# The norm ahead of a short convolution, with its root taken out of the matrix product: a two-block model on one Trainium2 core

## The reference, cut to what matters

```
def rmsnorm(x, w):
    y = x * rsqrt(mean(x * x, axis=-1) + 1e-6)
    return y * w

def shortconv_layer(h, w_in, conv_w, w_out):          # h is rmsnorm(x, norm_w[1])
    gate_b, gate_c, u, z = split(h @ w_in, 4, axis=-1)
    y = gate_b * causal_depthwise_conv(gate_c * u, conv_w)      # three taps
    return (y * silu(z)) @ w_out                                # added to x

x = x + hybrid_layer(rmsnorm(x, norm_w[0]), ...)
x = x + shortconv_layer(rmsnorm(x, norm_w[1]), ...)
return rmsnorm(x, final_norm_w)
```

## Time and profile before

| | |
|---|---|
| median of 3 runs | 3177.91 us (3171.27 to 3179.65) |
| the profiled execution: time, span | 3177.86 us, 3176.0 us |
| granted TensorE clock, mean | 0.982 |
| PE busy over the span | 2973.5 us (94%) |
| DVE, ACT, POOL busy | 2127.7 us (67%), 1550.3 us (49%), 87.7 us (3%) |
| HBM over the span | 171 GB/s |

### The profile page before, as it was taken

One profiled execution on the slowest core, in us unless ns is written; L12 is line 12 of the kernel. 1 busy time (PEld: TensorE's weight loads), 2 busy tenths in 40 slices (PEclk: granted clock), 3 DMA queues, 4 the chain that ended last, 5 costly groups with the idle time before them and its releaser, 6 DMA issues.

```text
span 3176.0 us, 53423 instructions
## 1 busy us (share of the span) xinstructions
PE 2973.5 (94%) x20420; PEld 2675.5 (84%) x20420; DVE 2127.7 (67%) x3042; ACT 1550.3 (49%) x2155; POOL 87.7 (3%) x113
## 2 busy tenths in 40 slices
PE   6989999987999998999799999999997899999998
PEld 6978888875988887777789999999997788888887
DVE  5766666665567778888666766776675665666655
ACT  4444444432455555777544544554453444444443
POOL 0000000000000000000000000000001000000000
PEclk9999999998999999999899999999998999999999
DMA  5423333320678887999434444444442455555554
GB/s 197 149 90 119 121 115 117 120 77 25 170 240 271 271 264 267 341 326 368 151 128 146 156 141 139 149 148 141 142 160 82 153 185 179 185 184 184 183 183 138
DMA packets 232514, 548.09 MB, mean 173 GB/s; under 512 B 17280, under 2 KB 99456, under 8 KB 232320
## 3 DMA queue, kind: packets, MB, share of 16 engines
q1 hardware_dynamic: 230240, 539.54, 51.4%
q0 software_dynamic: 1936, 5.64, 0.7%
q10 hardware_dynamic: 144, 0.19, 0.0%
HBM read 540.05 MB, written 2.10 MB: 171 GB/s over the span
## 4 chain that ended last, share of the span: by engine, by line
PE 63%; issue 26%; DVE 8%; ACT 3%; POOL 0%; DVEq 0%; ACTq 0%; POOLq 0%
PE gp L506 13%; PE gp L493 11%; PE gp L494 10%; PE gp L495 10%; PE gp L508 6%; PE pm L578 3%; DVE arena L2054 2%; PE pm L566 2%; DVE w_lo L1854 1%; ACT w_hi L1285 1%; PE pm L556 1%; DVE arena L1878 1%; DVE h_both L1866 0%; ACT h_both L1319 0%; PE pm L1205 0%
## 5 line engine op out<-in xcount | busy, mean ns | idle before, releaser
L1854 DVE TENSOR_TENSOR w_lo<-stage,w_hi 128x1024 fp32r<-128x1024 f32 x1018 | 1234.9, 1223 | 607.7 <-ACT w_hi L1285 597.4
L1285 ACT ACTIVATE w_hi<-stage 128x1024 fp32r<-128x1024 f32 x1018 | 1063.7, 1055 | 764.5 <-PE gp L495 318.1
L493 PE MATMUL gp<-h_both,w_hi 128*128 128x256 f32 x2896 | 860.5, 297 | 39.3 <-DVE h_both L1866 15.5
L494 PE MATMUL gp<-h_both,w_hi 128*128 128x256 f32 x2896 | 822.3, 284 | 0.0
L495 PE MATMUL gp<-h_both,w_lo 128*128 128x256 f32 x2896 | 822.1, 284 | 0.0
L493 PEld LDWEIGHTS gp<-h_both,w_hi 128*128 128x128 f32 x2896 | 557.8, 193 | 64.9 <-DVE h_both L1866 18.4
L494 PEld LDWEIGHTS gp<-h_both,w_hi 128*128 128x128 f32 x2896 | 558.6, 193 | 3.1 <-issue 1.7
L495 PEld LDWEIGHTS gp<-h_both,w_lo 128*128 128x128 f32 x2896 | 557.5, 193 | 0.0
L506 PE MATMUL gp<-h_both,w_hi 128*128 128x512 f32 x1536 | 541.7, 398 | 15.4 <-DVE h_both L1866 8.2
L508 PE MATMUL gp<-h_both,w_lo 128*128 128x256 f32 x1536 | 430.2, 280 | 0.0
L506 PEld LDWEIGHTS gp<-h_both,w_hi 128*128 128x128 f32 x1536 | 288.8, 188 | 88.9 <-DVE h_both L1866 10.0
(11 more groups left out here) (520 smaller groups left out, 4138.1 us busy)
## 6 DMA issues: line engine op xcount, KB each, us to landing
stage<-in_stream SPq DMA_DIRECT2D x1018, 512.0 KB, 4.4
x<-in_x SPq DMA_DIRECT2D x4, 512.0 KB, 6.0
arena<-c POOLq DMA_DIRECT2D x16, 128.0 KB, 2.2
out<-arena SPq DMA_DIRECT2D x4, 512.0 KB, 2.6
arena<-in_lora POOLq DMA_DIRECT2D x8, 192.0 KB, 2.8
arena<-arena POOLq DMA_DIRECT2D x16, 64.0 KB, 2.5
c<-in_c POOLq DMA_DIRECT2D x1, 896.0 KB, 4.9
c<-in_c SPq DMA_DIRECT2D x1, 704.0 KB, 12.9
```

Of the source, the lines that this page charges most:

```text
L493: T.matmul(o, w_hi[:, slot, w], hi[:, k, :], start=first[t], stop=False)
L494: T.matmul(o, w_hi[:, slot, w], lo[:, k, :], start=False, stop=False)
L1285: A.activation(w_hi[:, slot, :], stage[:, k, :], ACT.Copy).then_inc(s_hi, 1)
L1854: V.tensor_tensor(w_lo[:, slot, :], stage[:, sub % SLOTS, :], w_hi[:, slot, :].bitcast(F32), ALU.subtract).then_inc(s_lo, 1)
```

## The change

What PE multiplies is no longer the normed input but `x` times the norm's vector alone. It is split in its two parts during the fold, block by block, as soon as the blocks of `x` are complete. The root comes in later: after each unit of the short convolution DVE multiplies the emptied result by `n_rs` (b and z) or by its square `rs_sq` (c, which carries the root of u as well).

- ACT (`gained`): a copy with the norm's vector as scale writes `h_hi` block by block, 16 of them; for blocks 0 to 7 one more such copy into `xg`.
- POOL (`low_gained`): the low parts of blocks 0 to 7, `xg` less `h_hi`, among its sums of squares, which are now written out (`sum_more`).
- DVE (`low_gained`): the low parts of blocks 8 to 15 in one instruction each. `norm(3)` leaves it, with 16 L1878 and four 1024-wide L1866, and so do ACT's four 1024-wide L1319.
- PE: the first unit comes ahead of `norm_sum(3)`, which stands between the first and the second unit.
- DVE in each turn: for j = 0 and 1 a multiplication after the addition, linked; for j = 3 a multiplication of z by `n_rs`, which waits for the addition, and on whose end (`s_sc_z`) ACT's silu now waits. These are nine instructions of 128x256 more in a turn.
- Two semaphores are shared with others (`s_out`, `s_ab_kd`), with no work added.

```diff
@@ gpsimd
-            sum_blocks(3, SUMMED[3], ACC[3])
+            def low_gained(first, count):
+                for kt in range(first, first + count):
+                    pool.wait_ge(sem("s_hhi"), 12 + kt + 1)
+                    ins = G.tensor_tensor(h_lo[:, kt, :], xg[:, kt, :], h_hi[:, kt, :].bitcast(F32), ALU.subtract)
+                    if kt % 4 == 3:
+                        ins.then_inc(sem("s_hlo_pool"), 1)
...
+            low_gained(0, 4)
+            sum_more(1, 4)
+            low_gained(4, 4)
+            sum_more(4, SUMMED[3])
@@ tensor
-            norm_sum(3)
...
                     if first and n == 0:
+                        pe.wait_ge(s_evac[1], EV_SC[1] - 1)
                         for q in range(4):
                             hf_, cut = q // 2, q % 2 * SUB // 2
-                            pe.wait_ge(sem("s_hlo"), 12 + q + 1)
+                            if q < 2:
+                                pe.wait_ge(sem("s_hlo_pool"), q + 1)
+                            else:
+                                pe.wait_ge(sem("s_hlo"), 12 + q - 1)
                             wide_half(...)
+                        norm_sum(3)
@@ scalar
+            def gained(first, count):
+                for kt in range(first, first + count):
+                    if kt < 8:
+                        A.activation(xg[:, kt, :], x[:, kt, :], ACT.Copy, scale=vec("norm2", KT + kt))
+                    A.activation(h_hi[:, kt, :], x[:, kt, :], ACT.Copy, scale=vec("norm2", KT + kt)).then_inc(sem("s_hhi"), 1)
+
             for w, (first, count) in enumerate(FOLD2):
                 fold2(DN_H, w)
                 if w == 5:
                     act.wait_ge(sem("s_rt_in"), 4)
-                    square(12, 2)
+                    gained(12, 2)
                 act.wait_ge(s_evac[1], EV_SC[1] - 5 + w)
                 if w == 5:
-                    square(14, 2)
+                    gained(14, 2)
+                    square(12, 4)
                 else:
+                    gained(first, count)
                     square(first, count)
...
-            norm(3)
-            act.wait_ge(sem("s_hlo"), 16)
+            inverse_root(3)
...
-                        act.wait_ge(s_evac[k], EV_SC[k] + n // 3 + 1 + 4 * i)
+                        act.wait_ge(sem("s_sc_z"), 3 * i + bb + 1)
@@ vector
+                if w == 4:
+                    low_gained(*FOLD2[3])
             fold2(DN_H, 5)
+            low_gained(*FOLD2[4])
...
+            low_gained(*FOLD2[5])
-            merge(3, 14, 12, 13, 1)
+            merge(3, 16, 12, 13, 1)
...
-            norm(3, VEC["norm2"] + KT)
+            dve.wait_ge(sem("s_nrs"), 4)
+            link(V.tensor_tensor(rs_sq, n_rs, n_rs, ALU.mult))
...
                     V.tensor_tensor(o, o, gp[:, k, 0:S], ALU.add).then_inc(s_evac[k], 1)
-                    if j == 2:
-                        dve.wait_ge(s_evac[k], EV_SC[k] + n // 3 + 1 + 4 * i)
-                        link(V.tensor_tensor(o, o, q_c[:, bb, :], ALU.mult))
+                    dve.wait_ge(s_evac[k], EV_SC[k] + n // 3 + 1 + 4 * i)
+                    if j < 3:
+                        link(V.tensor_tensor(o, o, (n_rs, rs_sq, q_c[:, bb, :])[j], ALU.mult))
                     if j == 3:
+                        V.tensor_tensor(o, o, n_rs, ALU.mult).then_inc(sem("s_sc_z"), 1)
```

More of the change, by code:

```diff
@@ L341, in program @@
         (q_b, q_c, q_cu, q_z, q_a), _ = areas(0, [(3, S), (3, S), (3, S + 2), (3, S), (3, S)])
+        (rs_sq, xg), _ = areas(KT * S + S, [(S,), (8, S)])
         def sc_part(j, bb):
@@ L403, in _ @@
             for q in range(4):
-                sp.wait_ge(sem("s_hf"), 4 * 4 + q + 1)
-                sp.dma_start(out[:, 4 * q:4 * q + 4, :], hf[:, 4 * q:4 * q + 4, :]).then_inc(sem("s_out"), 16)
-            sp.wait_ge(sem("s_out"), 16 * 4)
+                sp.wait_ge(sem("s_hf"), 4 * 3 + q + 1)
+                sp.dma_start(out[:, 4 * q:4 * q + 4, :], hf[:, 4 * q:4 * q + 4, :]).then_inc(s_x[q], 16)
+            for q in range(4):
+                sp.wait_ge(s_x[q], 2 * 16)
         @block.gpsimd
@@ L472, in _, with sum_more @@
                 turn2(i, i == DN_H - 1)
-            sum_blocks(3, SUMMED[3], ACC[3])
+            def low_gained(first, count):
[4 more added lines that the diff above has]
+                        ins.then_inc(sem("s_hlo_pool"), 1)
+            def sum_more(first, end):
+                for k in range(first, end):
+                    pool.wait_ge(sem("s_sq"), KT * 3 + k + 1)
+                    if k > 1:
+                        pool.wait_ge(sem("s_acc"), ACC[3] + k - 1)
+                    G.tensor_tensor(n_rs, n_rs if k > 1 else hf[:, 0, :], hf[:, k, :], ALU.add).then_inc(sem("s_acc"), 1)
+            low_gained(0, 4)
+            sum_more(1, 4)
+            low_gained(4, 4)
+            sum_more(4, SUMMED[3])
             pool.wait_ge(s_evac[0], EV_SC[0])
             pool.wait_ge(s_evac[1], EV_SC[1])
-            pool.wait_ge(sem("s_hlo"), 4 * 4)
+            pool.wait_ge(sem("s_nrs"), 4)
             G.memset(q_cu[:, :, 0:2], 0.0).then_inc(s_zero, 1)
@@ L1080, in _ @@
                 if j == 2:
-                    pe.wait_ge(sem("s_ab_kd"), 1)
+                    pe.wait_ge(sem("s_ab_ac"), 2)
                     transposes([(pm[:, 0, c * P:(c + 1) * P], gb[:, c * P:(c + 1) * P]) for c in range(NT)], sem("s_ab_T"))
@@ L1653, in _ @@
             act.wait_ge(sem("s_ab_dv"), 2)
-            A.activation(gb[64:80, 0:P], g_x[0:16, 0:P], ACT.Exp).then_inc(sem("s_ab_kd"), 1)
+            A.activation(gb[64:80, 0:P], g_x[0:16, 0:P], ACT.Exp).then_inc(sem("s_ab_ac"), 1)
             for j in range(6):
@@ L2462, in _ @@
             V.tensor_scalar(nbeta, gtok[:, :, 32:48], -1.0, None, ALU.mult)
-            dve.wait_ge(sem("s_ab_ac"), 2)
+            dve.wait_ge(sem("s_ab_ac"), 3)
             V.tensor_scalar(n_low, con("incl"), -1.0, 1.0, ALU.mult, ALU.add).then_inc(sem("s_ab_tok"), 1)
@@ L2642, in _, with low_gained @@
                 chain.turn(8, turn2, i)
+            def low_gained(first, count):
+                for kt in range(first, first + count):
+                    dve.wait_ge(sem("s_hhi"), 12 + kt + 1)
+                    ins = V.scalar_tensor_tensor(h_lo[:, kt, :], x[:, kt, :], vec("norm2", KT + kt), h_hi[:, kt, :].bitcast(F32),
+                                                 ALU.mult, ALU.subtract)
+                    if kt % 4 == 3:
+                        ins.then_inc(sem("s_hlo"), 1)
             for w in range(5):
@@ L2692, in shortconv @@
                         lower(y_lo[:, 3 * i + bb, :], y_hi[:, 3 * i + bb, :], q_a[:, bb, :], s_y)
-            chain.loop(8, 15, shortconv)
+            chain.loop(8, 21, shortconv)
             out_turn = project(U_SOUT)
```

## The result

The changed kernel takes 3187.57 us (median of 12 runs, 3180.57 to 3193.93), the kernel before 3176.44 us beside it (12 runs, 3171.27 to 3180.20): a ratio of 1.0034, with a 95% interval of 1.0025 to 1.0042, some 11 us slower. The forecast was 3182.5 us, 4.6 us slower than before, in a range of 3172 to 3194. The profiled execution of the changed kernel is its fastest, 3180.57 us. Its fold begins 5.9 us earlier in the span than that of before, behind a part of the program in which only two semaphores differ. So I compare stretches, not spans.

The account below looks back on a forecast made before the run. PE, busy 94% of the span, was taken as the bound, so only its idle time counts: 3177.9 - 3.8 (head) + 8.4 (turns) = 3182.5 us; own range 3177 to 3188, all cases 3172 to 3194.

Parts of the forecast that it names:

- The sign and the place: Whole kernel: 4.6 us slower, with 3.8 us gained in the head and 8.4 us lost in the turns.
- POOL is not last: Head: POOL's sums end at about 2472, before the merges; the rival that POOL is last, 3184 us, had chance 0.06.
- the slower rival: Turns: each burst costs instruction and hand-over in series, 0.8 us, 19 us over 24 bursts, 3193 us; chance 0.17.
- The cost at nothing for j = 0 and 1: Turns: these multiplications stand where DVE waits on ACT, so cost nothing; without that cover 21.6 us over 48.
- 0.45 us per burst: Turns, j = 3: the z multiplication makes everything behind it in DVE's serial run 0.12 + 0.33 = 0.45 us later.
- The reserve of 0.15 in the slow pace: Turns, j = 3: at PE's slow pace three subs take 8.47 us, leaving the burst 0.15 us of reserve.
- the mixture: Turns: share of PE's fast (0.347) and slow (0.353) pace; 69.75 us a turn taken, 1.05 more, 8.4 in eight.
- The rival that the burst is covered: Turns: DVE's run hides the multiplication, so turns cost 0 to 2 us, total 3174 to 3176; chance 0.15.
- The head's 3.8 us: Head, fold to second unit's end: PE ends the second unit at 2485.5 against 2489.3, 3.8 us gained.
- the length of a step in the fold: Head: ACT's and DVE's work in series, 0.54 + 1.07 + 1.15 + 0.77 = 3.53 us per step of two blocks.
- The paragraph on POOL: Head: 8 subtractions beside 11 sums end at about 2472; if all are slow, 2479.1 and a gain of 2.1 us.
- full clock for quarter 3 and the sum: Head: PE's clock taken as full there; at 0.50 through both the gain would be 2.0 us.

Follow-up runs that it names:

- no_z: Changed kernel without the multiplication of z by the root at j = 3 and DVE's wait ahead of it: 3176.95 us, 0.9998 of the kernel before.
- z_alone: Kernel before with only the z multiplication at j = 3 added, DVE's wait ahead of it and silu waiting for it: 3188.6 us, 1.0035.
- low_dve: Changed kernel with all 16 low parts of the input on DVE and without ACT's eight copies to `xg`: 3180.39 us, 1.0007 of the kernel before.
- thin_sums_dve: Changed kernel with all 16 input low parts on DVE, ACT's copies kept, POOL's sums cut to 8 of 256 columns: one run, 3177.75 us.
- one_table: Changed kernel with silu's activation table loaded once, ahead of the turns: 3177.36 us, 0.9993 of the kernel before.
- thin_sums: Changed kernel with POOL's eleven sums cut to 8 of 256 columns, waits and order kept: 3184.74 us, 1.0022 of the kernel before.
- no_bc: Changed kernel without the multiplications at j = 0 and 1 (gates b and c): 3188.7 us, 1.0041 of the kernel before.
- b_last: Changed kernel with a channel group's units in order c, u, z, b, first tap at j = 2, gate b's root multiplied into y: 3171.06 us, 0.9960.

## Why the prediction was right, and where its sizes were off

**The sign and the place: right.** The head gains a little, the turns lose more, and POOL is not last: its sums ended at 2466.2 in the span of after, before the merges at 2471.39. The time lies inside the range, 5 us above the forecast, on the side of the slower rival. By the stretches of the profiles the change costs 10.9 - 2.4 = 8.5 us against the 4.6 of the sum; the median's 11 has an interval of some 8 to 13.

**The cost at nothing for j = 0 and 1: right**, shown by no_z. Beside the z multiplication they add nothing to PE's waits (20.1 us in the turns after, 20.2 in z_alone). The turns themselves differ (70.06 and 69.74), but low_dve, with the same turns as after, has 69.92: this is the pace of the next paragraph.

**0.45 us per burst: right in kind and size**, 0.46 on DVE, 0.47 in PE's time (1.40 / 3). The reserve of 0.15 in the slow pace was right too. Timeline of PEld after, a wait behind a stretch of each pace:

```profile
2571.26 0.19 PEld L525 LDWEIGHTS gp<-h_both,w_hi 128*128 128x128 f32 x1 [0.39 <-DVE w_lo L1884]
```

```profile
2664.18 0.19 PEld L525 LDWEIGHTS gp<-h_both,w_hi 128*128 128x128 f32 x1 [0.49 <-DVE w_lo L1884]
```

In the timelines of PE of after and of z_alone every stretch of 64 tiles between two waits of the turns runs at one of two paces, 0.3467 or 0.3533 us a tile. Of the first two waits of a turn after, those behind a slow stretch are 0.33 to 0.40 us, those behind a fast one 0.49 to 0.53. The two turns of after that are slow throughout take 70.30 and 70.27, where the prediction has 70.2. A turn that is fast throughout is not in it; one of thin_sums_dve takes 69.48, where the prediction has 69.4.

What was off is the mixture: "more frequent stalls may let PE fall back to the fast pace more often, so I take 69.75, 1.05 us a turn, **8.4 us lost**". PE did not fall back more often. Before, the mean pace of the six turns makes some 7 of 18 parts fast; after, 5 of their 18 stretches are. With that mixture the prediction's own two lengths give 70.0, and the turns measured 70.06: 1.40 more than before, 11.2 us in eight. In z_alone 10 of the 18 are fast, and its turns have 69.74; its 1.08 agrees with the prediction by that mixture. What sets the pace of a stretch is open, and so is whether z_alone's mixture is more than chance.

The rival that the burst is covered fell (23 waits in the turns). The slower rival's 0.8 us a burst fell as well: the burst cost 0.47, and the time went towards that rival by the mixture of paces and the head.

The Trainium skill ("ScalarE: Activation LUTs", What ACT_TABLE_LOAD costs) gives a table load about 1283 ns and a drain of some 1380 ns, 2.66 us in all. The rows of after agree with the first only: the instruction ahead ends at 2474.49, the load starts at 2474.59, the next instruction at 2475.88. At the end of a turn the load was worth (13.7 - 3.7) / 7 = 1.4 us of PE's waits, by one_table.

**The head's 3.8 us: right in kind, too large.** It measured 2.4, and the missing 1.4 is the three low parts that took 1.77 to 1.80 us: 3 x 0.55 = 1.65, by thin_sums, whose head gains 4.0. The step that failed is the length of a step in the fold, "1.07 (split to low part) + 1.15 (L1854 to L2481)". It took DVE's duration from a trace in which DVE started first. The paragraph on POOL weighed the same contention, but for POOL's side alone, "1.62 where DVE ran a low part", and put the gain of the head at 2.1 if POOL were late; POOL was not late, DVE was. ACT's 24 copies at 0.40 are as worked out.

The Trainium skill ("SBUF — State Buffer", SBUF: two separate sides) says that of a DVE instruction with two SBUF inputs and a GpSimd one that reads SBUF, the one that starts first has the shared ports for its whole duration and the other blocks. Both directions are in the rows of after, 1.66 for POOL's 0.73 where DVE began 0.16 us ahead and 1.77 for DVE's 1.23 where POOL began 0.03 us ahead, so the trace agrees. The two experiments show that POOL's sums are the cause; that the first to start has its way is read from these rows, and no run moves a start alone. I had used the rule for the engine that lost before, and not asked who would start first after.

**The clock.** Windows of after, the head in three parts (columns as in the earlier trace rows):

```profile
2433.70:2456.70 23.00, 17.50 (x120) 17.09 (x120) 6.95 (x7) 11.98 (x23) 10.47 (x14) 0.87 0.22 69
2456.70:2463.50 6.80, 5.74 (x25) 5.61 (x26) 4.36 (x6) 2.81 (x6) 3.70 (x4) 0.50 0.24 77
2463.50:2478.30 14.80, 10.20 (x53) 7.84 (x52) 9.84 (x17) 10.14 (x17) 1.58 (x3) 1.00 0.33 109
```

It fell to 0.50 at the 5 us wait, for 6.8 us, where before it was at 0.50 from the seam to 2476.2. I took full clock for quarter 3 and the sum, and that held: from 2463.5 on it is 1.00.

## What to carry to other kernels

An instruction costs what the engine that is waited for loses. Here 48 of 72 multiplications cost nothing and 24 of the same size cost 11 us, because these stood in a serial run ahead of two splits; parting the run over three units won back the 11 and 6.7 more, with as many instructions. So before moving work out of one stage, look for the longest serial run where it goes, and ask whether the operands that come last can be made to come earlier.

Where two engines exclude each other, a duration in the trace holds only for the order in which they started there. When a change shifts one of them, price both orders.

## What was not expected of the hardware

- The same instruction of DVE (128x1024, float32, two inputs in SBUF) takes 1.23 us alone, or where it begins ahead of POOL, and 1.77 to 1.80 where one of POOL's 128x256 additions began 0.02 to 0.03 us ahead of it. With additions of 8 columns it takes 1.22 to 1.26. Such an addition took 1.15 instead of 0.20 where DVE had begun 0.13 us ahead (thin_sums, 2464.25).
- The granted clock fell to 0.50 for 3.4 us three times in the turns of no_bc, behind waits of PE of 1.82 and 1.95 us, though PE was otherwise busy. Two other waits of 1.82 there have no fall behind them, and in the turns of after, with waits of up to 1.72, there is none. What decides is open.
- A run with PE never waiting (b_last) takes 671.6 us for the rest against 678.3 before, 6.7 less, where the seven waits before had 9.5 together. Some 2.8 us of them are given back by PE's pace: counted in the timeline of PE, all 1512 tiles behind the head run at 0.3533 us, the slow one of the two, where before more than a third ran at the fast one. Why there are two paces is as open as it was.
